# The end of the output and down projections of a two-layer encoder trunk: the last three weight units, in place of the last two, taken chunk by chunk

## The reference, cut to what matters

```python
merged = (gate_a * jnp.einsum("bte,ed->btd", o_dn, w_branch_a)
          + gate_b * jnp.einsum("bte,ed->btd", o_sw, w_branch_b))
mix = jnp.einsum("btd,de->bte", merged, w_out)                    # output projection, 1024 x 1024
x = layer_norm(DN_ALPHA * x + mix, ln1_g[l], ln1_b[l])
gate, up = jnp.split(jnp.einsum("btd,df->btf", x, w_gate_up[l]), 2, axis=-1)
down = jnp.einsum("btf,fd->btd", jax.nn.silu(gate) * up, w_down[l])  # down projection, 2816 x 1024
x = layer_norm(DN_ALPHA * x + down, ln2_g[l], ln2_b[l])
```

## Time and profile before

| | |
|---|---|
| median of 3 runs | 2601.8 us (2597.61 to 2605.43) |
| the profiled execution | 2598.42 us, span 2596.6 us |
| mean granted TensorE clock | 0.981 |
| PE busy | 2422.8 us, 93% of the span |
| DVE, POOL, ACT busy | 44%, 44%, 30% |

### The profile page before, as it was taken

How to read it: one execution, slowest core, us unless ns; L and a number is a source line. 1 busy time by engine, 2 the same in 40 slices (tenths; PEclk the granted TensorE clock), 3 DMA queues, 4 the chain that set the end, 5 groups by cost and what they waited for, 6 DMA issues and landing times.

```text
span 2596.6 us, 35628 instructions
## 1 busy us (share of the span) xinstructions
PE 2422.8 (93%) x14240; PEld 1998.1 (77%) x14240; DVE 1145.5 (44%) x2066; ACT 789.1 (30%) x2114; POOL 1134.9 (44%) x674
## 2 busy tenths in 40 slices
PE   8999999988988989999999999999889898999997
PEld 6877877777877778888778778778778777788885
DVE  4666677653333251110156666766533335411103
ACT  3644433453322021110045444434543221211100
POOL 4543232323323646666545432332332246566665
PEclk9999999999999999999999999999999999999999
DMA  3221111111112323333222111111111133233332
GB/s 129 90 66 42 38 50 44 40 38 41 41 33 98 106 73 97 98 98 97 91 98 82 58 49 38 46 41 38 46 41 41 33 106 113 74 97 97 114 94 85
DMA packets 53252, 181.69 MB, mean 70 GB/s; under 512 B 7392, under 2 KB 8032, under 8 KB 53088
## 3 DMA queue, kind: packets, MB, share of 16 engines
q1 hardware_dynamic: 44496, 160.71, 20.1%
q10 hardware_dynamic: 8592, 18.69, 2.3%
HBM read 169.94 MB, written 4.19 MB: 67 GB/s over the span
## 4 chain that ended last, share of the span: by engine, by line
PE 76%; DVE 13%; ACT 5%; issue 3%; DMA 1%; POOL 1%; ACTq 0%; DVEq 0%; SPq 0%; POOLq 0%
PE PS L527 20%; PE PS L528 19%; PE PS L529 19%; PE PS L887 3%; DVE Y L1599 3%; PE PS L943 2%; DMA w_raw<-stream 1%; PE PS L761 1%; PE PS L848 1%; ACT DT L1144 1%; DVE att L1666 1%; PE PS L705 1%; ACT pr L1274 1%; PE PS L772 1%; DVE V L1587 1%
## 5 line engine op out<-in xcount | busy, mean ns | idle before, releaser
L488 POOL TENSOR_SCALAR wh<-w_raw 128x1024 fp32r<-128x1024 f32 (+1 forms) x301 | 323.5, 1075 | 1350.6 <-DMA w_raw<-stream 1350.2
L491 POOL TENSOR_TENSOR wl<-w_raw,wh 128x1024 fp32r<-128x1024 f32 (+1 forms) x301 | 722.6, 2401 | 25.1
L527 PE MATMUL PS<-xh,wh 128*128 128x512 f32 x1664 | 689.4, 414 | 19.6 <-POOL wl L491 6.9
L529 PE MATMUL PS<-xl,wh 128*128 128x512 f32 x1664 | 658.3, 396 | 0.0
L528 PE MATMUL PS<-xh,wl 128*128 128x512 f32 x1664 | 657.0, 395 | 0.0
L527 PEld LDWEIGHTS PS<-xh,wh 128*128 128x128 f32 x1664 | 318.7, 192 | 79.1 <-POOL wl L491 8.2
L529 PEld LDWEIGHTS PS<-xl,wh 128*128 128x128 f32 x1664 | 317.4, 191 | 69.9
L528 PEld LDWEIGHTS PS<-xh,wl 128*128 128x128 f32 x1664 | 319.5, 192 | 55.2
L1500 DVE SCALAR_TENSOR_TENSOR conv_acc<-PS,cw,conv_acc 128x510 f32<-128x510 f32 x192 | 143.9, 749 | 120.5 <-ACT conv_acc L1113 115.3
L1848 DVE TENSOR_TENSOR hf<-sg,PS 128x512 f32<-128x512 f32 x44 | 30.2, 687 | 357.7 <-PE PS L529 357.7
L527 PE MATMUL PS<-wh,hh 128*128 128x512 f32 x352 | 138.9, 395 | 3.4 <-POOL wl L491 3.4
(11 more groups left out here) (249 smaller groups left out, 4084.3 us busy)
## 6 DMA issues: line engine op xcount, KB each, us to landing
w_raw<-stream SPq DMA_DIRECT2D x300, 512.0 KB, 3.5
x<-x_in ACTq DMA_DIRECT2D x6, 512.0 KB, 7.2
qx<-qx ACTq DMA_DIRECT2D x48, 64.0 KB, 2.0
raw<-raw ACTq DMA_DIRECT2D x32, 64.0 KB, 2.1
ln_g<-ln_rows ACTq DMA_DIRECT2D x4, 512.0 KB, 4.3
ln_b<-ln_rows ACTq DMA_DIRECT2D x4, 512.0 KB, 5.8
x_park<-x ACTq DMA_DIRECT2D x4, 512.0 KB, 4.9
x<-x_park ACTq DMA_DIRECT2D x4, 512.0 KB, 6.6
```

The lines of the kernel that those rows point to most:

```text
L488: nc.gpsimd.tensor_scalar(wh[s][:, w], w_raw[s][:, w], 1.0, 1.0, ALU.mult, ALU.mult).then_inc(w_hi_done, 1)
L491: nc.gpsimd.tensor_tensor(wl[s][:, w], w_raw[s][:, w], wh[s][:, w].bitcast(F32), ALU.subtract).then_inc(split_done, 1)
L527: mm(o, ah, bh, start=first, stop=False)
L529: return mm(o, ah, bl, start=False, stop=last)
```

## The change

The tail takes the last three units instead of two. Three slots hold them, so all three slots stay occupied until the last half of chunk 3. The loop ahead of it ends one unit earlier. In chunk 0, PE waits for each of the three units just before it uses it.

```diff
-                for i in range(npairs - 1):
-                    for s in range(2):
-                        w_slot = unit_ready(l * PAIRS + first_pair + i, s)
-                        pe.wait_ge(ready, ready_count + i * 2 + s + 1)
-                        for c in (2, 3, 0, 1):
...
-                w_slots = [unit_ready(l * PAIRS + first_pair + npairs - 1, s) for s in range(2)]
+                last = range(npairs * 2 - 3, npairs * 2)
+                for u in range(npairs * 2 - 3):
+                    w_slot = unit_ready(l * PAIRS + first_pair + u // 2, u % 2)
+                    pe.wait_ge(ready, ready_count + u + 1)
+                    for c in (2, 3, 0, 1):
...
                 pe.wait_ge(ready, ready_count + npairs * 2)
-                tile = npairs * 2 - 2
                 for c in range(CHUNKS - 1):
-                    for j in range(2):
+                    for u in last:
+                        w_slot = slot_of(l * PAIRS + first_pair + u // 2, u % 2)
+                        if c == 0:
+                            unit_ready(l * PAIRS + first_pair + u // 2, u % 2)
                         for half in range(2):
-                            ins = half_of(tile + j, w_slots[j], c, half, False, j == 1)
+                            ins = half_of(u, w_slot, c, half, False, u == last[-1])
                     ins.then_inc(y_mm, 1)
 
                 for half in range(2):
-                    for j in range(2):
-                        ins = half_of(tile + j, w_slots[j], CHUNKS - 1, half, False, j == 1)
+                    for u in last:
+                        ins = half_of(u, slot_of(l * PAIRS + first_pair + u // 2, u % 2), CHUNKS - 1, half, False,
+                                      u == last[-1])
                         if half == 1:
                             ins.then_inc(unit_done, 1)
```

More of the change, by code:

```diff
@@ L593, in token_units @@
-                w_slots = [unit_ready(l * PAIRS + first_pair + npairs - 1, s) for s in range(2)]
+                last = range(npairs * 2 - 3, npairs * 2)
[3 more added lines that the diff above has]
+                    for c in (2, 3, 0, 1):
+                        if u == c == 0:
+                            pe.wait_ge(freed, freed_count)
+                        for half in range(2):
+                            ins = half_of(u, w_slot, c, half, u == 0, False)
+                    ins.then_inc(unit_done, 1)
```

## The result

The changed kernel took 2617.95 us in the median of 5 runs (2614.9 to 2625.53); the kernel before, on the same chips, 2601.26 us (2593.67 to 2605.43). The ratio is 1.0067, with a 95% interval of 1.0047 to 1.0088: 17 us slower, 12 to 23. The forecast was +11.0 us, slower, and 2612.5 us with a range of 2603 to 2622.

A forecast was written before the change was run, and what follows sets the result against it. PE's own work was taken as the bound, only its idle time movable. Places 1 to 4 gave +4.1, +3.5, +3.0 and +0.4, together +11.0 us; forecast 2612.5 us, range 2603 to 2622.

The forecast's parts named there:

- The wait: Tails, chunk 0: PE resumes at the same moment with 60 matmuls left instead of 48, +2.8 us at each of four places.
- The clock: Matmuls behind the tail's longer wait run at half clock: +1.3 us in places 1, 2 and 4, +0.2 in place 3.
- The norm: Behind each tail, the last half's sum begins 0.2 us after T, PE's end, instead of 1.7: -1.5 us.
- The break behind the first three matmuls of the next stage: Next stage: PE starts earlier, breaks off after three matmuls, does the rest from T + 10.9; gain 0.6 us.
- Behind T, place 2: After T, the tail's end: PE's earlier start in the next stage leaves -0.6 us; 0 in places 1 and 3.
- Place 4: No next stage: last sum -1.5 us, scaling 0.3 us instead of 2.49, -2.2; with wait and clock +0.4 us.
- (b): Head start of 1.5 us comes through in places 1 to 3, clock costs nothing: +3.0, 2604.8 us; chance 0.18.
- (c): Faster: transposes wait 0.9 instead of 2.41 us, PE keeps full clock, half-clock stretch behind 924 goes; 2601 us, chance 0.05.
- (a): The forecast: four times, wait grows 2.8 us and clock falls, norm gives back little; bad end +19.9 us, chance 0.77.

## Why the prediction was right

**The wait.** "PE resumes at the same moment, but with 60 matmuls to do in place of 48": right in places 1, 2 and 4, counted from the first matmul of unit 5, to 0.2 us; in place 3 PE resumed 8.9 us behind it, before 9.5. The waits were 4.2, 4.1, 5.7 and 4.1 us (both of chunk 0 added; in places 2, 3 and 4 the first was 0.28, 0.36 and 0.23), where 4.5 and 6.5 were forecast. The short pause for unit 6 I had not seen; it moved nothing, because the wait for unit 7 ends when POOL's split ends. The term, 11.2 us in all, stands on the two runs that changed only the cover: with 24 matmuls of it the loss was 1 us, and 6 more in the kernel before gave 6.5 us.

**The clock.** The mechanism was right and the term too small: 4.1 us forecast. The tails grew by 17.0 us in the traces, of which 11.2 are the 48 matmuls that lost their cover, so 5.8 are the clock: 2.5, 1.6, 0.3 and 1.4 us in places 1 to 4, where 1.3, 1.3, 0.2 and 1.3 were forecast. The run with the wait filled gives 5.7 by its trace. It is place 1 above all that was mis-sized. There, 13 matmuls ran in 5.4 us where 23 would, 2.3 us lost, more than the 1.5 that I had set as the bound. I had taken one half-clock stretch of 3.4 us as the most that a wait brings. One of 5.4 us and more was in view (924 to 931 in the earlier trace rows), and I used it for a rival, but not as the bound here. A nearer row for the wait itself was in the same trace and not used: in place 3 before, PE waited 2.51 us for the fourth unit, and the 8 matmuls from 2231.70 on ran at half the clock. Of the stretch behind the fourth unit in place 1 (1.6 us) the forecast has no term at all. Besides, half-clock stretches far from any edit come and go from trace to trace. The changed kernel's has this one, in which before 16 matmuls ran at full clock:

```profile
104.00:107.20 3.20, 3.20 (x10) 0.50 0.00 0
```

Four of the nine experiments' traces have it too, two of them with the two-unit tail, so it is no work of the change. Such a stretch also lies at 2087 to 2091, among the 3.8 us between place 2 and place 3. For this part of the +20.3 us of span I give no cause.

**The norm.** -1.5 us for the last sum: right (the sum came 0.04 us behind T where 1.7 was computed before, the last scaling at T + 3.4 where T + 3.5 was forecast). That it would not come through in place 1: right as well. The break behind the first three matmuls of the next stage, the second start at T + 10.3 (forecast 10.9), the end of the `xl` chain at T + 19.3 (forecast 19), and the fourth unit, which is split only when DVE's gain and offset end, all came as written. What was left of the head start, 1.5 us in place 1 where I had 0.6, went into that wait. It was longer than before, but PE came out of it at T + 31.7 and T + 32.0 against 31.6 and 31.7 in places 1 and 3. What the forecast had no word for is the clock behind that wait in place 1, 1.6 us.

**Behind T, place 2.** -0.6 forecast, -1.1 measured. PE began for good at T + 10.5 and not at T + 12.4 as before, a gain of 1.9 us, but then ran at half the clock for longer:

```profile
1317.40:1322.40 5.00, 5.00 (x12) 0.50 0.00 0
```

Before, it was one stretch of 3.4 us with 8 matmuls there. Twelve in 5 us cost 2.2 us where 8 in 3.4 cost 1.5, so 0.7 of the 1.9 are lost again; the first matmul of the next product shows the 1.1 us that are left. The 0.6 had been T + 10.9 against 11.5, three matmuls at full pace behind T + 10.8. But before, those three ran at half the clock in place 1 (924.58 to 926.06, 1.5 us), and in place 2 PE broke off behind them too (the 0.68 us at 1306.34). So the gain was larger than I had worked out, and it was the longer half-clock stretch that brought the term back near the forecast: luck.

**Place 4.** -3.7 against T forecast, -3.0 measured. The scaling took 1.21 us and not 0.3, since POOL was not quite done (and 0.3 was too little in any case, as its 0.54 us without POOL in place 2 shows; the 2.49 of the other bound were not its own length):

```profile
2606.85 2.34 POOL L510 TENSOR_TENSOR x<-x,ln_b 128x1024 f32<-128x1024 f32 x1
...
2608.26 1.21 DVE L1786 TENSOR_SCALAR x<-x,ln_mv,ln_rs 128x512 f32<-128x512 f32 x1
```

POOL ended at T + 4.3, where I had T + 3.1. DVE's order is fixed: `factors(0)` stands behind `summed(1)`, and with chunks 4.2 us apart DVE waits for chunk 1 before it finishes chunk 0:

```profile
2596.59 1.22 DVE L1741 SCALAR_TENSOR_TENSOR x<-x,PS 128x1024 f32<-128x1024 f32 x1 [1.24 <-PE PS L529]
```

So chunk 0's scaling, and POOL behind it, came 1.2 us later than the 6.1 us behind chunk 0 that I had carried over from before. The scaling again ends 0.28 us behind POOL's instruction, as in the earlier trace rows: here 2609.19 and 2609.47. That the one who comes second is blocked for the other's whole instruction is what the Trainium skill says ("SBUF — State Buffer", "SBUF: two separate sides"); the trace agrees, and the 0.28 us are the trace's alone.

**The rivals.** (b) and (c) needed the half clock to stay away from the waits or to leave the norm; neither happened. The other condition of (b), which hung on a few tenths, was met for the scaling in places 2 and 3 and missed in place 1; the break behind the first three matmuls came in all three. The bounds of (a), 19.9 us at its bad end, hold what was measured.

In sum: cover 11.2, clock in the tails 5.8, place 4 -3.0, and behind T 1.6 in place 1, -1.1 in place 2 and 0.3 in place 3 makes 14.8 us, with 17 (12 to 23) measured. The forecast's sum was 11.0: its mechanism held and its clock term was too small, by 1.7 us in the tails and 1.6 behind place 1.

## What to carry to other kernels

Before work is reordered at the end of a stage, count what stands between the release of a buffer and the first use of what is loaded into it, and compare it with the latency of load and preparation (here 7.3 us against 12 matmuls, 2.8 us). Every microsecond of cover that is moved behind the wait was paid in full here, and again through the clock of TensorE where the wait became long. An earlier start for the engines behind is worth looking for only once the wait is gone: with one more buffer the same three-unit tail was part of a kernel that is 22 us faster, of which 16 came with the buffer alone.

## What the runs showed of the hardware that was not expected

Matmuls of a zero matrix in bf16, 17 in 3.84 us, in a wait of some 4 us were enough that the matmuls behind it ran at full clock (23 in 5.4 us, where 13 ran without them), in a kernel whose other products there are float32.

A GpSimd instruction that came up while DVE ran a block of instructions with two inputs in SBUF waited there for the whole block and not for one instruction: the fourth unit's high part took 3.39 us in place of 1.05, until the last of eight such instructions had ended. This is no rule: in the kernel before, ahead of place 3, a block of eight such DVE instructions and POOL's splits took turns, and both took longer than by themselves (2.4 and 1.2 us):

```profile
2161.49 3.25 POOL L491 TENSOR_TENSOR wl<-w_raw,wh 128x1024 fp32r<-128x1024 f32 x1
2162.40 3.42 DVE L1378 TENSOR_TENSOR x<-x,ln_g 128x1024 f32<-128x1024 f32 x1
```

What decides between the two was not followed up. Breaking up the block was worth 9 us (6 to 13) in the kernel before, where the waits in its trace had led me to expect 2 to 5; where the rest comes from was not followed up either.
